# A hybrid RWKV-7 / S5 layer on one core: input tiles asked for one stage earlier, position rows spread by TensorE, one table record loaded one stage earlier

## What is computed

```
xs = x_sample + grid_pos_embed(n_tok, D_MODEL)        # latent tokens only

pe = concatenate([broadcast_to(e_r[:, None], (rows, GRID_W, d // 2)),     # same for the 64 tokens of a grid row
                  broadcast_to(e_c[None],    (rows, GRID_W, d // 2))])    # same in every grid row

h = rms_norm(x, norm1_g) * (1.0 + sc1) + sh1
z = h @ w_in                     # its last 512 columns are u, the input of the S5 group
y_s = s5_mix(z[..., OFF_U:], ...)    # diagonal state space scan in both directions
```

## Time and profile before

| what | value |
|---|---|
| median of 3 runs | 2148.41 us (2148.17 to 2150.22) |
| the profiled execution's own time | 2147.13 us |
| its span | 2145.3 us |
| PE busy | 1841.6 us (86%) |
| DVE busy | 1031.2 us (48%) |
| ACT busy | 635.7 us (30%) |
| POOL busy | 525.1 us (24%) |
| front stage, from / to | 0 / 62.3 us |
| first norm | 62.3 / 119.9 us |
| u stage | 119.9 / 230.7 us |
| state space stage | 230.7 / 399.3 us |

### The profile page before, as it was taken

One profiled execution on the slowest core, in us unless ns is written; L12 is line 12 of the kernel. 1 busy time (PEld: TensorE's weight loads), 2 busy tenths in 40 slices (PEclk: granted clock), 3 DMA queues, 4 the chain that ended last, 5 costly groups with the idle time before them and its releaser, 6 DMA issues. The chain is left out here.

```text
span 2145.3 us, 55493 instructions
## 1 busy us (share of the span) xinstructions
PE 1841.6 (86%) x24160; PEld 1152.4 (54%) x24160; DVE 1031.2 (48%) x1685; ACT 635.7 (30%) x1209; POOL 525.1 (24%) x596
## 2 busy tenths in 40 slices
PE   6289587779999648999999389799999999999988
PEld 1244476335555337999988244454545455454533
DVE  8789556510688834555544744222222222222276
ACT  0511244332555413444444213231203021120202
POOL 0510000033111023555544533231203111120110
PEclk9589689899999878999999699899999999999999
DMA  6664332421244354434343232221111121111122
GB/s 234 221 209 162 139 110 79 150 64 50 75 149 149 125 181 131 111 104 115 107 140 100 97 114 89 99 79 40 40 40 40 40 79 40 40 40 40 40 78 89
DMA packets 172361, 215.87 MB, mean 101 GB/s; under 512 B 41034, under 2 KB 127050, under 8 KB 170446
## 3 DMA queue, kind: packets, MB, share of 16 engines
q1 hardware_dynamic: 172244, 214.18, 30.5%
HBM read 151.63 MB, written 60.42 MB: 99 GB/s over the span
## 5 line engine op out<-in xcount | busy, mean ns | idle before, releaser
L89 PE MATMUL psum<-arena 128*128 128x384 bf16 (+1 forms) x2028 | 710.5, 350 | 71.4 <-PEq L500 14.7
L90 PE MATMUL psum<-arena 128*128 128x384 bf16 (+1 forms) x2028 | 709.6, 350 | 0.0
L91 PE MATMUL psum<-arena 128*128 128x384 bf16 (+1 forms) x2028 | 709.3, 350 | 0.0
L1629 PE MATMUL psum<-arena 64*64 64x64 f32 x9216 | 343.4, 224 | 24.5 <-issue 19.8
L89 PEld LDWEIGHTS psum<-arena 128*128 128x128 bf16 x2028 | 200.7, 99 | 267.0 <-issue 39.6
L1629 PEld LDWEIGHTS psum<-arena 64*64 64x64 f32 x9216 | 310.7, 136 | 43.0 <-issue 32.2
L1623 PE MATMUL psum<-arena 64*64 64x64 f32 (+2 forms) x6336 | 284.5, 239 | 47.7 <-DMA arena<-xrec 37.5
L91 PEld LDWEIGHTS psum<-arena 128*128 128x128 bf16 x2028 | 201.1, 99 | 178.3 <-issue 8.0
L90 PEld LDWEIGHTS psum<-arena 128*128 128x128 bf16 x2028 | 201.2, 99 | 171.1 <-issue 6.6
L1623 PEld LDWEIGHTS psum<-arena 64*64 64x64 f32 x6336 | 244.3, 136 | 53.4 <-issue 50.1
L1769 ACT ACTIVATE arena<-psum 128x192 f32<-128x192 f32 (+1 forms) x600 | 174.5, 337 | 267.8 <-PE psum L1629 191.4
(11 more groups left out here) (274 smaller groups left out, 2055.2 us busy)
## 6 DMA issues: line engine op xcount, KB each, us to landing
arena<-in_w_ff SPq DMA_DIRECT2D x16, 2048.0 KB, 7.8
arena<-in_w_ada SPq DMA_DIRECT2D x12, 2048.0 KB, 8.5
arena<-xrec SPq DMA_DIRECT2D x72, 320.0 KB, 3.4
arena<-s_tab SPq DMA_DIRECT2D x8, 1600.0 KB, 7.4
x<-arena SPq DMA_DIRECT2D x18, 512.0 KB, 3.4
xrec<-arena SPq DMA_DIRECT2D x4, 2304.0 KB
arena<-xrec SPq DMA_DIRECT2D x72, 128.0 KB, 2.6
arena<-x SPq DMA_DIRECT2D x18, 512.0 KB, 3.3
```

Of the source, the lines that this page charges most:

```text
L89: nc.tensor.matmul(out, whi, xhi, start=first, stop=False)
L90: nc.tensor.matmul(out, wlo, xhi, start=False, stop=False)
L91: return nc.tensor.matmul(out, whi, xlo, start=False, stop=last)
L1629: done = nc.tensor.matmul(out[half[1 - h]], lhs[half[h]], rhs[half[h]], start=first, stop=last)
```

## The change

In the front stage SP no longer loads the u weights. It asks for the first four x tiles, the column positions and two DMAs of position rows: partition 0 of `M.pos_rows` gets the first token's row of each latent tile, partition 64 the row of token 64, and GpSimd first sets the whole 128x4096 buffer to zero. SP waits for all seven. The `w_ada` buffers of this stage lie on `M.hi` and `M.lo`, which the first norm fills later.

In the first norm SP loads the u weights first and then only x tiles. The row positions of tile b come from TensorE: one f32 product of `M.head_ones` (128x128, two 64x64 blocks of ones) with `M.pos_rows[:, b]` gives a 128x512 PSUM tile with each token's row; it is called R(b) below. R(0) and R(1) stand ahead of the loop, R(b + 2) stands behind T(b). VectorE's left add reads this PSUM tile. ScalarE's rounding of the u weights is cut into four 128x1024 pieces in its turns 2 to 5, and GpSimd's four pieces move to its turns 3 to 6.

In the u stage SP asks for record 0 of `s5_tab` in its third group, once the products are done and the first sends have landed, into the place that `rec[0]` has in the next stage. There `load(0)` is left out, and the waits for records are renumbered.

```
@@ stage_front
-    wst = [A.take(KD, 512) for _ in range(2)]
+    wst = [v.rearrange("p k t -> p (k t)").bitcast(F32)[:, 0:KD * 512].rearrange("p (k n) -> p k n", k=KD) for v in (M.hi, M.lo)]
...
-            sp.dma_start(M.wu, ins["w_in"][:, :, OFF_U:OFF_U + DS]).then_inc(ev("w_u"), 16)
-            sp.wait_ge(ev("w_u"), 16)
+            for b in range(4):
+                sp.dma_start(M.xt[b], ins["x"][b]).then_inc(ev("x"), 16)
+            sp.dma_start(M.columns, ins["pos"][0][:, D // 2:D]).then_inc(ev("x"), 16)
+            sp.wait_ge(ev("rows_zero"), 1)
+            for row in (0, 64):
+                sp.dma_start(M.pos_rows[row:row + 1], ins["pos"][0:LB, row:row + 1, 0:D // 2].rearrange("b r n -> r b n")).then_inc(ev("x"), 16)
+            sp.wait_ge(ev("x"), 16 * 7)
+
+        @block.gpsimd
+        def _(pool):
+            nc.gpsimd.memset(M.pos_rows, 0.0).then_inc(ev("rows_zero"), 1)
@@ stage_norm1, sync
-                if b < LB:
-                    sp.dma_start(rows[b % 4], ins["pos"][b][:, 0:H]).then_inc(ev("loaded", b % 4), 16)
-            load(0)
-            sp.dma_start(columns, ins["pos"][0][:, H:D]).then_inc(ev("columns"), 16)
-            for b in range(1, 4):
-                load(b)
+            sp.dma_start(M.wu, ins["w_in"][:, :, OFF_U:OFF_U + DS]).then_inc(ev("w_u"), 16)
@@ stage_norm1, scalar
-            nc.scalar.activation(M.wu_hi, M.wu, ACT.Copy).then_inc(ev("wu_hi"), 1)
...
+                if 2 <= b < 6:
+                    ks = slice(2 * b - 4, 2 * b - 2)
+                    act.wait_ge(ev("w_u"), 16)
+                    nc.scalar.activation(M.wu_hi[:, ks], M.wu[:, ks], ACT.Copy).then_inc(ev("wu_hi"), 1)
@@ stage_norm1, gpsimd
-                if b < 4:
-                    ks = slice(2 * b, 2 * b + 2)
-                    pool.wait_ge(ev("wu_hi"), 1)
+                if 3 <= b < 7:
+                    ks = slice(2 * b - 6, 2 * b - 4)
+                    pool.wait_ge(ev("wu_hi"), b - 2)
@@ stage_norm1, tensor
+            def rows(b):
+                if b >= LB:
+                    return
+                need(pe, ev("added"), 2 * (b - 2) + 1 if b >= 2 else 0)
+                nc.tensor.matmul(ps[:, ROWS + b % 2, :], M.head_ones, M.pos_rows[:, b, :], start=True, stop=True).then_inc(ev("rows"), 1)
+            rows(0)
+            rows(1)
...
                 last.then_inc(ev("transposed"), 1)
+                rows(b + 2)
@@ stage_norm1, vector
-                dve.wait_ge(ev("loaded", b % 4), 32 * (b // 4) + 32)
-                if b == 0:
-                    dve.wait_ge(ev("columns"), 16)
+                need(dve, ev("loaded", b % 4), 16 * (b // 4))
+                dve.wait_ge(ev("rows"), b + 1)
                 x = xt[b % 4]
-                nc.vector.tensor_tensor(x[:, 0:H], x[:, 0:H], rows[b % 4], ALU.add).then_inc(ev("added"), 1)
+                nc.vector.tensor_tensor(x[:, 0:H], x[:, 0:H], ps[:, ROWS + b % 2, :], ALU.add).then_inc(ev("added"), 1)
@@ stage_u, sync
+                if i == 2:
+                    sp.wait_ge(ev("product"), CH + 1)
+                    for q in range(2):
+                        sp.wait_ge(ev("sent", q), 32)
+                    sp.wait_ge(ev("rot_out", 0), 32)
+                    sp.dma_start(M.first_rec, ins["s5_tab"][0]).then_inc(ev("rec"), 16)
...
+            sp.wait_ge(ev("rec"), 16)
@@ stage_s5
-            load(0)
...
-                pe.wait_ge(ev("rec", b % 3), b // 3 * 16 + 16)
+                need(pe, ev("rec", b % 3), (b + 2) // 3 * 16)
```

More of the change, by code:

```diff
@@ L170, in stage_front @@
     th = A.take(KD, 2)
-    sc = M.silu
-    wst = [A.take(KD, 512) for _ in range(2)]
+    sc = M.silu[:, :, 0:2]
+    wst = [v.rearrange("p k t -> p (k t)").bitcast(F32)[:, 0:KD * 512].rearrange("p (k n) -> p k n", k=KD) for v in (M.hi, M.lo)]
     par = A.take(3, G)
@@ L372, in stage_norm1 @@
     keep = A.at
-    xt = [A.take(D) for _ in range(4)]
-    rows = [A.take(D // 2) for _ in range(4)]
-    columns = A.take(D // 2)
+    xt, columns = M.xt, M.columns
+    ROWS = 4
     junk = A.take(D)
@@ L398, in _ @@
                 else:
-                    sp.wait_ge(ev("loaded", b % 4), 32 * (b // 4) + 16)
+                    sp.wait_ge(ev("loaded", b % 4), 16 * (b // 4))
                 sp.dma_start(ins["x1"][b], xt[b % 4]).then_inc(ev("stored", b % 4), 16)
@@ L415, in squares @@
                 else:
-                    act.wait_ge(ev("loaded", b % 4), 32 * (b // 4) + 16)
+                    act.wait_ge(ev("loaded", b % 4), 16 * (b // 4))
                 need(act, ev("rstd"), b - 3)
@@ L882, in _ @@
                 cos, sin = (rot[b % 3][:, n].unsqueeze(1).broadcast_to([P, 2, QUAD * NC_]) for n in range(2))
-                dve.wait_ge(ev("rec", b % 3), b // 3 * 16 + 16)
+                need(dve, ev("rec", b % 3), (b + 2) // 3 * 16)
                 dve.wait_ge(ev("x"), 2 * b + 2)
@@ L2497, in program @@
     M.wu_hi, M.wu_lo = A.take(KD, DS, dt=BF16), A.take(KD, DS, dt=BF16)
+    M.first_rec = M.arena.t[:, keep_u + CH * DS:keep_u + CH * DS + S5_REC]
+    after_u = A.at
+    M.xt = [A.take(D) for _ in range(4)]
+    M.columns, M.pos_rows = A.take(D // 2), A.take(LB, D // 2)
     stage_front(nc, M, ins)
     stage_norm1(nc, M, ins)
+    A.at = after_u
     stage_u(nc, M, ins)
```

## The result

| | before | after |
|---|---|---|
| median of 21 runs each, taken together | 2147.0 us (2141.46 to 2153.82) | 2153.82 us (2151.55 to 2158.3) |
| profiled execution / its span | 2147.13 / 2145.3 | 2154.07 / 2152.3 |
| granted clock, mean | 0.922 | 0.924 |

The ratio is 1.0035, with a 95% interval of 1.0028 to 1.0043. The forecast was 2154.9 us and slower, by +6.5 us in one profiled execution against another; the spans differ by 7.0. Single runs of one kernel lie up to 12 us apart, so the terms are read from stage borders, not from totals.

The account below looks back on a forecast made before the run. Stages run in sequence, no engine full over the first norm, VectorE bounding the u stage. Terms 0.7 - 4.8 + 44.8 + 2.1 - 29.5 - 6.8 = +6.5 us gave 2154.9 us, range 2150.5 to 2158.5.

Parts of the forecast that it names:

- Memset: Front stage: GpSimd's zeroing may hold up VectorE's chain; 0.7 us lost, the middle between 0 and 1.3.
- The step: First norm, from T(b), eight transpositions, to T(b + 1): 7.46 us, bounds 7.3 and 7.7; six steps 44.8 us.
- Rival D: First norm: the loop is partly hidden, a step costs 6.5 to 6.9 us, total 2149 to 2152; chance 0.1.
- The collisions: First norm, adds 6 and 7: VectorE's right add waits for GpSimd's u weight piece; 2.1 us lost, bounds 0 and 2.1.
- Rival A: First norm: right adds do not collide with GpSimd's pieces; 2.1 us less, 2152.8 us; chance 0.18.
- Behind T(6): First norm's end: from the seventh tile's transpositions to the last GpSimd operation stays 12.64 us.
- u stage: SP's load of record 0 costs one issue of 0.43 us and VectorE's chain keeps its length; cost 0.
- The record: State space stage: turn(0) no longer waits for its load; 6.8 us won, bounds 5 and 8.
- Rival C: State space stage: the moved record gains little, so +10.3 us, 2158.7 us; chance 0.1.
- The clock: First norm: TensorE stays at 1.2 GHz (PEclk 0.50), since pauses drop any rise a burst brings.
- the ring: First norm: R(b + 2) behind T(b) closes a loop through add, squares and scaling to T(b + 1); 7.46 us a round.
- Rival B: First norm: TensorE runs at 2.4 GHz in the rounds, a step takes 5.8 us, total 2141.3 us; chance 0.05.

Follow-up runs that it names:

- the two experiments on the record: Kernel before with only record 0 loaded in the u stage: 2137.14 us, ratio 0.997; changed kernel with that part taken back: 2159.54 us, ratio 1.0069.
- the run with the rows by transfers: Kernel before with early x tiles, moved record and later u weight pieces, position rows still loaded by DMA, no R or memset: 2136.97 us, ratio 0.9941.
- the first experiment: Changed kernel with R(b + 2) moved ahead of T(b) on TensorE: 2132.2 us, ratio 0.9944 to the kernel before.

## Why the prediction was right

The sign, the size and the mechanism came out; term by term:

- **Memset**: +0.7 taken, +0.82 measured in the chain. The rule of the Trainium skill ("SBUF — State Buffer", "Who interferes with whom") agrees in kind with this trace: the one-input operations were locked out until the memset's end, the two-input one was not. By the full lock the text had put 1.3. That was too much on two counts: the memset ended at 4.26 and not 4.4, and the text let the held-up operation start 0.2 behind the memset's end, while L281 and L249 both ended 0.05 behind it and the chain went on. The 0.7 was the middle between no wait and the full one; that it came so near is in part luck, since what happened was the full wait at a smaller price.
- **Start of the first norm**: T(0) predicted 7.5 us behind the stage's start, measured 7.60.
- **The step**: 7.46 predicted, with bounds 7.3 and 7.7; measured 7.51, 7.33, 7.39 and 7.59. T(0) to T(6) predicted 46.9 with the collisions, measured 46.83. Rival D, a loop that is partly hidden, falls.
- **The collisions**: 2 x 1.05 predicted in adds 6 and 7, 2 x 0.92 measured in the same two. The add does end about 0.55 behind GpSimd's piece, as inferred from the left add of the earlier trace rows; the piece came 0.13 us earlier against the add than worked out. Rival A falls.
- **Behind T(6)**: 12.64 us kept to the start of the last GpSimd operation, measured 130.64 - 117.63 = 13.01, 0.37 more. This and 0.1 ahead of it are the norm's miss (13.1 against 12.6). The prediction gave GpSimd's pieces 1.2 us of slack because it looked at the next `low` alone; the piece of turn 5 has another instruction behind it in the list, the reciprocal root of tile 8, which ScalarE's scaling waits for:

```profile
120.94 2.15 POOL L460 TENSOR_TENSOR arena<-arena 128x1024 bf16<-128x1024 f32 x1
...
123.06 0.53 POOL L449 TENSOR_TENSOR arena<-arena 128x1 f32<-128x1 f32 x1
...
123.62 1.15 ACT L433 ACTIVATE arena<-arena 128x1024 f32<-128x1024 f32 x1 [0.25 <-POOL arena L449]
...
124.82 1.97 PE L475 MATMUL psum<-arena 128*128 128x128 f32 x8 [1.72 <-ACT arena L433]
```

T(8) starts 3.69 us behind T(7), where it was 3.33 before.

- **u stage**: 0 predicted, +1.0 measured. It isn't the moved load, as the two experiments on the record show (111.05 with it alone, 112.0 without it but with the rest). The load's own issue took 0.87 us where 0.43 was taken. Part of the +1.0, 0.6 us, is VectorE's wait for the first send (1.14 instead of 0.55). It goes with the row products and their buffer: the u stage takes 110.8 to 111.05 us in the four profiled runs without them, the run with the rows by transfers among them (110.8, wait 0.51), and 111.4 to 112.4 in the eight with them. Why that send lands later stays open.
- **The record**: 6.8 predicted at turn(0), 6.81 measured; 6.2 by the runs of the part alone. Rival C falls.
- **The clock**: 0.50 throughout was wrong, the stage's mean is 0.60. What the forecast rested on held all the same: the transpositions and R's of the ring ran at 1.2 GHz but for parts of a few (a T of 1.78, an R of 1.72), since the rises came in the pauses. The Trainium skill ("TensorE: Matmul & The Clock Gate", part 1) was used for "a burst may lift it, the pause drops it again"; this trace agrees only in part. The lift came, but behind the burst and in four of seven pauses, and in the rows shown the clock stayed up through the pause and was down again in the next burst. Rival B, priced at 2141.3, needed bursts that themselves ran at 2.4 GHz. That happened once the ring was open and the pauses short, as in the first experiment, and for single products where each R was done twice (1.02 us), not in this kernel.

The total is nearer than its terms. The misses were +0.2 (front), +0.5 (first norm), +1.0 (u stage), -0.5 (state space stage) and -0.6 (all that follows), 2.8 us without their signs and 0.6 with them. The upper end of the range, 2158.5, isn't what it names for it either: the memset in full and the step at 7.7 add 0.6 and 1.4 to 2154.9, which is 2156.9. The result lies inside both.

The one thing that the prediction didn't ask is whether the ring was needed: it priced the order as given. Moving the product one place would have been the first thing to say.

## What to carry to other kernels

When work moves from a transfer to an engine with an in-order list, draw the ring: what the new instruction stands behind, who waits for it, and who releases what it stands behind. If that closes, every round pays the whole ring, with each engine idle for about half of the time (busy for 31 to 35 of the 70.7 us here) and no busy share that tells it; here one call moved above the transpositions was worth 19.6 us of a 70.7 us stage. And start work for a next stage early where its engine idles: the record asked for one stage ahead gave its whole 6.8 us of waiting.

## What was unexpected

- TensorE's clock rose behind some of the bursts of 3.2 to 3.8 us (four of seven), was up in pauses with 0.00 us of work, and down again for the next burst. A stage's mean clock (0.60 here, 0.50 before) can thus rise without a matmul getting shorter; compare the lengths of the instructions, not the mean.
- A GpSimd memset of 4096 f32 columns takes 3.51 us and held up two of VectorE's 0.18 us one-input operations until its end, but not one with two inputs.
- The same program's state space stage took 168.5 and 166.2 us in two profiled executions, and its totals range over 10 us and more. A term under 2 us was only ever seen at a border or a single instruction.
